# The gate stage's opening in a hybrid recurrent trunk: norm waits later in VectorE's queue, lifts one pair later, a fourth gate buffer

## The reference, cut to what matters

```python
out_a = _rms(o, gdn_norm_w) * silu(g_z)         # branch 0; 1 and 3 in the same way, 3 with a sigmoid
out_c = _rms(y * silu(s_z), ssd_norm_w)         # branch 2: gated first, then normed
branches = stack([out_a, out_b, out_c, out_d])  # each 256 wide
up    = einsum('btnw,nwd->btnd', branches, w_branch)        # the lift: 256 -> 1024, 4 branches
gates = sigmoid(gate.reshape(B, T, 4, 1024))                # gate = h @ w_in[:, C_GATE:]
merged = einsum('btnd,btnd->btd', gates, up)
y = merged @ w_out
```

## Time and profile before

| what | value |
|---|---|
| median of three executions | 1176.51 us (1175.53 to 1179.0) |
| the profiled execution, its own time | 1176.42 us |
| its span, first to last instruction | 1174.6 us |
| outside the span | 1.8 us |
| mean granted TensorE clock over the span | 0.961 of full |
| PE busy | 1101.2 us, 94% of the span |
| PE idle in the opening, 442.8 to 520.1 us | four waits, 13.5 us |
| DVE busy | 820.2 us, 70% |
| ACT busy | 458.2 us, 39% |

### The profile page before, as it was taken

How to read it: one execution, slowest core, us unless ns; L and a number is a source line. 1 busy time by engine, 2 the same in 40 slices (tenths; PEclk the granted TensorE clock), 3 DMA queues, 4 the chain that set the end, 5 groups by cost and what they waited for, 6 DMA issues and landing times.

```text
span 1174.6 us, 26651 instructions
## 1 busy us (share of the span) xinstructions
PE 1101.2 (94%) x11347; PEld 1029.5 (88%) x11347; DVE 820.2 (70%) x1464; ACT 458.2 (39%) x686; POOL 11.6 (1%) x29
## 2 busy tenths in 40 slices
PE   5889979999999999789999999979999999999997
PEld 3589978887667888789999999969999999999997
DVE  1647967778667865678888885586888889763433
ACT  2534495721102315763343332145444434541121
POOL 0001100000000000000000000000000000000000
PEclk9889999999869989989999999989999999999999
DMA  9924421112557216113333334222233333233201
GB/s 302 273 80 102 101 73 38 38 39 83 157 161 211 83 38 166 39 37 73 99 101 101 104 99 149 73 72 73 73 107 84 98 109 97 79 105 90 87 14 77
DMA packets 191052, 116.99 MB, mean 100 GB/s; under 512 B 36650, under 2 KB 189351, under 8 KB 190678
## 3 DMA queue, kind: packets, MB, share of 16 engines
q1 hardware_dynamic: 190358, 115.16, 34.7%
q0 software_dynamic: 576, 0.14, 0.1%
HBM read 108.31 MB, written 6.96 MB: 98 GB/s over the span
## 4 chain that ended last, share of the span: by engine, by line
PE 71%; DVE 6%; ACT 2%; issue 1%; DVEq 1%; ACTq 1%; PEldq 0%; PEld 0%
PE ps L924 70%; PE ps L928 1%; DVEq L2294 1%; DVE scr_parts L2992 1%; DVE pj L2274 1%; DVE pj_parts L3300 1%; ACTq L2123 0%; DVE scr L2706 0%; ACT rstd L1879 0%; DVE scr L2778 0%; DVE Vr L3254 0%; ACT scr_parts L2069 0%; DVEq L2275 0%; DVE scr L2953 0%; ACT scr L1989 0%
## 5 line engine op out<-in xcount | busy, mean ns | idle before, releaser
L924 PE MATMUL ps<-high_parts,scr_parts 128*128 128x272 f32 x1396 | 315.8, 297 | 22.4 <-DVE scr_parts L2992 9.5
L924 PE MATMUL ps<-hT_parts,scr_parts 128*128 128x272 f32 x960 | 263.3, 294 | 1.2 <-DVE pj_parts L3300 1.2
L924 PEld LDWEIGHTS ps<-high_parts,scr_parts 128*128 128x128 f32 x1396 | 239.4, 195 | 25.2 <-issue 12.7
L924 PE MATMUL ps<-pj_parts,scr_parts 128*128 128x272 f32 x1560 | 249.0, 289 | 0.3 <-issue 0.3
L924 PE MATMUL ps<-high_parts,ring_parts 128*128 128x272 f32 x812 | 238.6, 294 | 0.0
L924 PEld LDWEIGHTS ps<-pj_parts,scr_parts 128*128 128x128 f32 x1560 | 217.1, 188 | 0.7 <-issue 0.7
L924 PEld LDWEIGHTS ps<-hT_parts,scr_parts 128*128 128x128 f32 x960 | 179.1, 193 | 1.4 <-DVE scr_parts L2992 1.4
L924 PEld LDWEIGHTS ps<-high_parts,ring_parts 128*128 128x128 f32 x812 | 157.8, 194 | 0.7
L2992 DVE TENSOR_TENSOR scr_parts<-ring,scr_parts 128x1024 fp32r<-128x1024 f32 (+1 forms) x38 | 52.7, 1392 | 84.2 <-ACT scr_parts L2016 83.0
L2016 ACT ACTIVATE scr_parts<-ring 128x1024 fp32r<-128x1024 f32 (+1 forms) x38 | 44.9, 1191 | 142.6 <-PE ps L924 142.5
L924 PE MATMUL ps<-scr 64*64 64x64 f32 (+6 forms) x2352 | 80.4, 233 | 3.1 <-DVEq L2294 1.9
(11 more groups left out here) (424 smaller groups left out, 1820.3 us busy)
## 6 DMA issues: line engine op xcount, KB each, us to landing
ring<-in_w_in_dram SPq DMA_DIRECT2D x62, 512.0 KB, 5.1
ring<-in_ffn_w_in_dram SPq DMA_DIRECT2D x44, 512.0 KB, 5.2
ring<-in_ada_w_dram SPq DMA_DIRECT2D x40, 512.0 KB, 5.9
ring<-in_ffn_w_out_dram SPq DMA_DIRECT2D x16, 384.0 KB, 3.5
ring<-in_ffn_w_out_dram SPq DMA_DIRECT2D x16, 320.0 KB, 4.2
pj<-in_ada_w_dram SPq DMA_DIRECT2D x8, 512.0 KB, 8.3
ring<-in_w_out_dram SPq DMA_DIRECT2D x8, 512.0 KB, 4.2
x_scratch<-scr SPq DMA_DIRECT2D x1, 2176.0 KB, 12.2
```

The lines of the kernel that those rows point to most:

```text
L924: return pe.matmul(out, lhsT, rhs, start=start, stop=stop, skip_group_check=True)
```

## The change

It moves entries within the queues of ACT, DVE and PE, gives the gate pairs a fourth buffer, and lets the lifts follow one pair later. No matmul, split or product is added or left out.

- `high(0)` goes ahead of ACT's last `read_group`, `low(0)` ahead of DVE's `g_outc11`, and PE waits for the last copy (`x_read`) itself before `product(0)`.
- On ACT the loop over products 0 to 5 is written out: `T4_hi` goes ahead of `high(5)`; the logarithms of branches 0 and 1 are both taken ahead of both exponentials; `high(7)`, `high_a(0)`, `gate_out(1)` and `high_s(0)` stand ahead of the logarithms of branch 3; the exponentials of branches 2 and 3 follow together. The four silus of the z tiles go behind `gate_out(3)`.
- On DVE each `branch_squares` goes behind more splits, `branch_scaled(2)`, `branch_scaled(3)` and all `branch_gated` go into units 0 and 1, so that only `T3_lo` is left behind the splits of unit 0.
- On PE no lift follows unit 0, lifts 2s - 2 and 2s - 1 follow unit s, eight instead of six lifts follow unit 13. `sigmoid_a(0)` waits for no branch, `sigmoid_a(1)` for two.
- Two tiles are split to high and low during units 4 and 6, four (2 to 5) behind unit 13; before, four during units 3, 5, 7 and 9.

```diff
-MERGED, MERGED_HI = [0, 1, 2, 3, 6, 7, 8, 9], [14, 15, 16, 17, 28, 29, 4, 5]
+MERGED, MERGED_HI = [0, 1, 2, 3, 6, 7, 8, 9], [28, 29, 20, 21, 24, 25, 4, 5]
...
-            return ((pj[:, 10, :], pj[:, 11, :]), (Er[:, :], Vr[:, :]), (pj[:, 28, :], pj[:, 29, :]))[p % 3]
+            return ((pj[:, 10, :], pj[:, 11, :]), (Er[:, :], Vr[:, :]), (pj[:, 16, :], pj[:, 17, :]), (pj[:, 14, :], pj[:, 15, :]))[p % 4]
...
+            pe.wait_ge(x_read, GROUPS)
             for k in range(M_WOUT):
...
             for s in range(SG):
                 unit(s)
-                lift(2 * s)
-                lift(2 * s + 1)
-            for j in range(2 * SG, 4 * KD):
+                if s:
+                    lift(2 * s - 2)
+                    lift(2 * s - 1)
+            for j in range(2 * SG - 2, 4 * KD):
                 lift(j)
...
+                if engine == "act" and chain == "x" and name == "read":
+                    if t == GROUPS - 1:
+
+                        rest.after(act, NT, "m_normc")
+                        hgrn.after(act, PAIRS[-1], "h_outc1")
+                        high(0)
+                    read_group(t)
...
             def sigmoid_a(s):
-                if s == 0:
-                    act.wait_ge(branch_ready, 4)
-                else:
-                    act.wait_ge(lin_read, 2 * s)
+                if s == 1:
+                    act.wait_ge(branch_ready, 2)
+                elif s:
+                    act.wait_ge(lin_read, 2 * s - 2)
...
+            high(2)
+            z_out(0)
+            high(3)
+            z_out(1)
+            act.wait_ge(t_ready, 1)
+            act.activation(g_T2_hi, g_T2_raw, ACT.Copy).then_inc(t_high, 1)
+            act.activation(g_T1_hi, g_T1_raw, ACT.Copy).then_inc(t_high, 1)
+            high(4)
+            z_out(2)
+            norm_logs(0)
+            act.wait_ge(t_ready, 2)
+            act.activation(g_T4_hi, g_T4_raw, ACT.Copy).then_inc(t_high, 1)
+            high(5)
+            z_out(3)
+            norm_logs(1)
+            norm_exps(0)
+            norm_exps(1)
+            high(6)
+            gate_out(0)
+            norm_logs(2)
+            high(7)
             high_a(0)
+            gate_out(1)
             high_s(0)
+            norm_logs(3)
+            norm_exps(2)
+            norm_exps(3)
 
             act.wait_ge(first_scaled, 1)
             gate_out(2)
             high_b(0)
             high_s4(0)
-            for z in (GZ, GZ + 1, HG, HG + 1):
-                act.activation(pj[:, z, :], pj[:, z, :], ACT.Silu).then_inc(z_ready, 1)
             act.wait_ge(w_done, M_WOUT)
...
             gate_out(3)
+            for z in (GZ, GZ + 1, HG, HG + 1):
+                act.activation(pj[:, z, :], pj[:, z, :], ACT.Silu).then_inc(z_ready, 1)
...
+                    if (chain, t, name) == ("g", PAIRS[-1], "g_outc11"):
+
+                        low(0)
                     next(gens[chain])
...
             low(4)
+            branch_squares(1)
+            low(5)
             branch_squares(2)
-            branch_scaled(0)
-            low(5)
-            branch_squares(3)
             dve.wait_ge(t_high, 3)
             dve.tensor_tensor(g_T4_lo, g_T4_raw, g_T4_hi.bitcast(F32), SUB).then_inc(t_split, 1)
+            branch_scaled(0)
+            low(6)
             branch_scaled(1)
             sums(0)
-            low(6)
-            branch_scaled(2)
+            branch_squares(3)
             low(7)
-            branch_scaled(3)
...
+                if s == 0:
+                    branch_gated(0)
+                    branch_gated(1)
+                elif s == 1:
+                    for n in (2, 3):
+                        branch_scaled(n)
+                        branch_gated(n)
+                if s:
+                    gate_times_lift(2 * s - 2)
+            for k in range(2 * SG - 3, 4 * KD):
                 gate_times_lift(k)
-            merged_low(4)
-            gate_times_lift(4 * KD - 1)
-            merged_low(5)
+                if k < 2 * SG + 1:
+                    merged_low(k - 2 * SG + 5)
```

More of the change, by code:

```diff
@@ L1990, in rest_act @@
                         yield
[L1992 to L1999, removed]
             def high(m, at=None, n_at=None):
@@ L2016, in high @@
                 act.activation(hi, src, ACT.Copy).then_inc(w_split_hi, 1)
-            rest.after(act, NT, "m_normc")
-            hgrn.after(act, PAIRS[-1], "h_outc1")
-            high(0)
+            gens = {"g": gdn_act(), "h": hgrn_act(), "s": rest_act()}
+            for chain, t, name, engine in order:
+                if engine == "act" and chain == "x" and name == "read":
[4 more added lines that the diff above has]
+                    read_group(t)
+                elif engine == "act" and chain == "x":
+                    weights_high(t, int(name[-1]))
+                elif engine == "act":
+                    next(gens[chain])
             high(1)
@@ L2103, in sigmoid_a2 @@
                 act.activation(sw_gate(s)[:, halves[1]], sw_gate(s)[:, halves[1]], ACT.Sigmoid).then_inc(gate_sig, 1)
[L2105 to L2129, removed]
@@ L2130, in _, with norm_logs, norm_exps @@
-            act.drain()
+            def norm_logs(n):
+                mid.begin(act, 0, f"o_rs{n}")
+                for f in range(2):
+                    act.activation(two(rms[n][f]), ps[:, 4 + 2 * f:6 + 2 * f, 0:HN], ACT.Ln,
+                                   scale=1.0 / (P if n == 2 else DK), bias=colp[:, 3:4])
+                act.drain().then_inc(mid_s, 1)
+            def norm_exps(n):
+                for f in range(2):
+                    act.activation(rms[n][f], rms[n][f], ACT.Exp, scale=-0.5)
+                act.drain().then_inc(rms_ready, 1)
@@ L2157, in _ @@
                     high(M_WOUT + 1)
-                if s % 2 == 1 and 3 <= s < 11:
-                    merged_high((s - 3) // 2)
+                if s in (4, 6):
+                    merged_high((s - 4) // 2)
                 sigmoid_b(s)
                 sigmoid_a2(s)
-            act.wait_ge(lin_read, 4 * KD - 2)
-            merged_high(4)
-            merged_high(5)
+            act.wait_ge(op_done, 7 * (SG - 1) + 6)
+            for d in range(2, 6):
+                merged_high(d)
             act.wait_ge(lin_done, 4 * KD - 3)
@@ L2969, in rest_dve, with low @@
                         yield
+            def low(m, at=None):
+                _, src = piece(m)
+                hi, lo = parts(m)
+                dve.wait_ge(w_split_hi, (m if at is None else at) + 1)
+                dve.tensor_tensor(lo, src, hi.bitcast(F32), SUB).then_inc(w_split, 1)
             gens = {"g": gdn_dve(), "h": hgrn_dve(), "s": rest_dve()}
@@ L2985, in _ @@
             done(mid)
[L2987 to L2992, removed]
             def freed(s, j):
@@ L3121, in whole @@
                 tt(out, h_hi[:, k, c].bitcast(F32), h_lo[:, k, c].bitcast(F32), ADD)
-            low(0)
             low(1)
@@ L3135, in _ @@
             low(3)
-            branch_squares(1)
             dve.wait_ge(q_out["mlstm"], 64)
@@ L3161, in _ @@
             low_a(0, upper, 4)
[L3162 to L3167, removed]
+            for n in range(2):
+                at = slice(2 * n, 2 * n + 2)
+                dve.wait_ge(t_high, 4 + n)
+                dve.tensor_tensor(T3_lo[:, at, :], g_T3_raw[n], T3_hi[:, at, :].bitcast(F32), SUB).then_inc(t_split, 1)
             def merged_low(d):
@@ L3195, in _ @@
                 prepare = s + 1 < SG
-                if s:
-                    gate_times_lift(2 * s - 1)
+                if s >= 2:
+                    gate_times_lift(2 * s - 3)
                 if prepare:
@@ L3218, in _ @@
                     low_a(s + 1, upper, 4)
[L3219 to L3222, removed]
+                if s in (4, 6):
+                    merged_low((s - 4) // 2)
+                if s == 0:
[8 more added lines that the diff above has]
+            for k in range(2 * SG - 3, 4 * KD):
                 gate_times_lift(k)
-            merged_low(4)
-            gate_times_lift(4 * KD - 1)
-            merged_low(5)
+                if k < 2 * SG + 1:
+                    merged_low(k - 2 * SG + 5)
             mid.begin(dve, 0, "upc")
```

## The result

The changed kernel takes 1166.97 us (median of nine executions, 1162.95 to 1170.86) beside 1177.57 us for the kernel before (nine executions, 1169.56 to 1182.46): the ratio is **0.9914, interval 0.9885 to 0.9942**. The profiled execution took 1166.01 us with a span of 1164.2 us; before it was 1176.42 and 1174.6. The forecast was 1165.8 us, 0.991 of the kernel before.

The account below looks back on a forecast made before the run. PE's matmuls, plus time PE stands or runs slow, were taken as the bound. Losses of 19.2 us fall to 0.5 + 1.5 + 6.0 + 0.6 = 8.6; gain 10.6 from 1176.42 gives 1165.8 us, range 1162.5 to 1170.5.

Parts of the forecast that it names:

- The loss before (19.2 us): Opening of the stage, kernel before: four PE waits, 13.5 us, plus 5.7 us of low clock behind them.
- Start, 0.5 us left: Ahead of `product(0)`: 0.5 of the 2.69 us PE wait remains, too short to lower the clock.
- Products 4 and 6, no wait: Ahead of products 4 and 6: PE's waits of 2.65 and 4.15 us go, splits covered by at least 5 us.
- T3_lo, 1.5 us: Unit 0, after its second seventh: PE waits 1.5 us for `T3_lo` in place of 4.0.
- Units 0 to 2, 6.0 us: DVE late for PE in units 0 to 2: 6.0 us of new waits, including 0.5 for hand-overs.
- The clock in these waits, 0 taken: Units 0 to 2: 0 us for clock falls; up to 4.2 us kept in the range; clock 0.50 would show it wrong.
- Tail, 0.6 us: Lifts at the stage's end: merged splits on DVE make lift 30 late by 0.6 us.
- A, the forecast: Whole kernel: the forecast holds, 1162.5 to 1169 us; chance 0.65.
- B (clock): Units 1 and 2: the clock falls and is not absorbed, whole kernel 1170 us; chance 0.15.
- C (the backlog hardly shows): Units 1 and 2: PE never waits for DVE there, gain 16.6 us, 1159.8 us; chance 0.08.
- E (waits only change places): Ahead of `low(5)`: the serial chain squares, sums, logarithm holds DVE, losses return, 1176.4 us; chance 0.03.
- F (DVE never catches up): Units 3 to 13: every unit waits for `third_side`; 1185 us at a DVE period of 16 us; chance 0.03.

Follow-up runs that it names:

- e5: Changed kernel with each norm's exponentials directly behind its logarithms on ACT, three table loads more; 1166.99 us, ratio to before 0.9895.
- e2: Changed kernel with `high(0)` and `low(0)` moved back to their old places, PE still waiting for the last copy; 1169.46 us, ratio to before 0.9955.
- e4: Changed kernel with lifts 2s and 2s+1 behind unit s as before, DVE's `gate_times_lift` two earlier; 1171.28 us, ratio to before 0.9947.
- e7: Changed kernel with `branch_scaled(2)`, `(3)` ahead of `low_b(0)` and `branch_gated(0)` moved behind `up_second(1)`; 1163.46 us, ratio to before 0.9848.
- e9: Changed kernel with `branch_scaled(2)`, `(3)`, all `branch_gated` ahead of `T3_lo`, silus ahead of `T3_hi`, lifts 2s, 2s+1 behind unit s; 1169.45 us, ratio to before 0.9942.
- e6: Changed kernel with `branch_scaled(2)` and `(3)` taken out of unit 1 and put ahead of `low_b(0)` on DVE; 1164.04 us, ratio to before 0.9866.

## Why the prediction was right, and what it mis-sized

**What bounds and where: right.** The sum was a gain of 10.6 us; the stage gave 9.76, and the profiled executions 10.4, of which 0.3 each lie ahead of the stage and behind it.

**The loss before (19.2 us): right, at most 0.5 too low.** The four waits are as read. The clock was taken at 1.4 us for each. The start alone gave 3.58 us for 2.69 - 0.49 = 2.20 of wait, so 1.4 for one fits. From the start of `product(0)` to that of unit 0's second seventh PE took 68.96 us before (445.51 to 514.47) and 57.76 after (442.99 to 500.75): 11.20 less, for two waits of 6.80, so 4.4 us for three falls of the clock.

**Start, 0.5 us left: right** (0.49, clock 1.00).

**Products 4 and 6, no wait: right,** and the cover was as large as said: `low(5)`, `low(6)` and `low(7)` end at 471.7, 479.8 and 487.5. Even three table loads more (`e5`) brought no wait there.

**T3_lo, 1.5 us: 1.01.** ACT's walk ended at 501.21 us (501.3 said) and DVE's at 503.33 (503.6).

**Units 0 to 2, 6.0 us: the right size, by parts that were not.** The printed waits are 0.36 + 1.72 + 2.45 = 4.5. The rest is in waits too short to be printed. From the start of the second seventh of unit 0 to that of unit 1 (500.75 to 513.75) PE took 13.0 us, and seven sevenths (10.6) with the two printed waits (1.4) make 12.0. One result after another is handed over just too late. The fifth seventh of unit 0 waits for ACT's `copy_first(0)`, which ends at 506.56, and starts 0.15 us later; at 0.126 us a matmul the fourth would have let it start at 506.53, and the profile prints no wait:

```profile
505.02 1.67 PE L924 MATMUL ps<-scr_parts 128*128 128x272 f32 x12
...
506.19 0.37 ACT L2091 ACTIVATE rstd<-ps 128x272 f32<-128x272 f32 x1
...
506.71 0.36 PE L924 MATMUL ps<-high_parts,scr_parts 128*128 128x272 f32 x1
```

From unit 1 to unit 2 another 0.4 us is missing (16.32 us between the second sevenths, for 14.2 + 1.72). My 0.5 for hand-overs should have been 1.4, while the printed waits came to less than I had worked out.

**The clock in these waits, 0 taken: the step that failed.** It fell behind the wait of 2.45 us and cost 1.8: 18.46 us lie between the second sevenths of units 2 and 3, against 14.2 + 2.45, and the two windows above account for 2.50 x 0.27 + 2.80 x 0.37 = 1.7 of it.

```profile
530.07 1.68 PE L924 MATMUL ps<-scr_parts 128*128 128x272 f32 x12
...
548.53 1.67 PE L924 MATMUL ps<-scr_parts 128*128 128x272 f32 x12
```

The granted clock was 0.50 from 540 to 542 us, which the prediction had listed among the signs of being wrong. The argument that slower sevenths only shorten the next wait did not hold, since this was the last wait. The bound of 1.4 us for a fall was also too low.

**Tail, 0.6 us: 0.24.** It is lift 30 that is held, as said.

**The sum after** is then 0.5 + 1.0 + 4.5 + 1.4 + 1.8 + 0.2 = 9.4 us in place of 8.6, and 19.2 - 9.4 = 9.8 is what the stage gave. The failed step adds 1.8 us and the waits that came out smaller take 1.0 back. That the forecast came within 1.2 us of the measured median is in part luck: the executions of the changed kernel alone spread over 8 us.

**The table loads.** In the changed kernel ACT starts an exponential 1.29 us after its load starts:

```profile
472.59 1.28 ACT L2118 ACT_TABLE_LOAD   x1
473.88 0.66 ACT L2118 ACTIVATE Er<-Er 128x544 f32<-128x544 f32 x1
```

**The rivals.** A, the forecast, came true. B (clock) came true in one wait of three. C (the backlog hardly shows) is refuted by 4.5 us of printed waits. E (waits only change places) is refuted by products 4 and 6. F (DVE never catches up): no wait of PE lies between unit 2 and the last lifts.

## What to carry to other kernels

Work that an engine does in the shadow of another's wait is not free to move: when the wait goes, list what that engine must do until its next hand-over, beside what the bound engine does in the same stretch; the difference is the new wait, here 4.5 us, and the places where the helping engine still stands (3.56 us at `low_b(0)`) are where to put the work. Order a helper's queue by when each result is needed, and do not put a product's operand behind a serial chain that passes through a third engine. In this kernel PE's waits in the stage of up to 1.72 us kept the clock and those of 2.45 us and more lost it, all but one, at 1.4 to 1.8 us each (2.3 behind the one of 9.6); so a single long wait is worth removing before the same total in short ones.

## What the runs showed of the hardware

**The same length of wait does not always cost the clock.** It fell behind waits of 2.65 and 2.69 us, behind 2.78 us in `e2`, and in three profiles behind the 2.45 us; it stayed at 1.00 behind 2.77 us in `e4`. The Trainium skill (page "TensorE: Matmul & The Clock Gate", section "Part 1: The HAM clock gate") says that the window in which PE's activity is watched is free-running and does not reset when a kernel starts, and explains with it why the first matmuls of a kernel reach full speed at a varying point. That the place of a wait decides in the same way is not shown here: the runs would allow it, but in `e4` other work, too, stands around the wait (lifts follow it, not a seventh).

**The profile's idle time of PE is too short.** In the sevenths matmuls start 0.126 us apart but are drawn 0.29 us long, so 0.16 us of each stop is hidden under the last one's modelled end. A stall below that is not printed at all; distances between equal landmarks show it.

**The spread of executions goes with the mixers' clock.** The granted clock from 200 to 440 us, in `e7`, the changed kernel and `e9`, whose mixers ended at 451.4, 442.5 and 438.1 us:

```profile
200.00:440.00 240.00, 227.63 (x4449) 187.50 (x4450) 170.09 (x388) 66.58 (x123) 0.00 (x0) 0.88 0.34 99
```

```profile
200.00:440.00 240.00, 226.76 (x4592) 188.25 (x4590) 175.01 (x404) 65.13 (x122) 0.00 (x0) 0.91 0.34 99
```

```profile
200.00:440.00 240.00, 226.18 (x4625) 188.26 (x4624) 177.58 (x408) 67.72 (x124) 0.00 (x0) 0.94 0.34 100
```

The program of the mixers is the same in all three kernels, and their end spreads over 13 us. In all eleven profiles the two go together: clock 0.94, end at 438.1 and 440.4 us; 0.91, 441.7 to 447.0; 0.90, 446.5; 0.88, 450.8 and 451.4. This is why `e6` and `e7` were profiled in spans of 1168.6 and 1168.7 us although their stages are 4 to 5 us shorter than the changed kernel's; what sets the clock there was not tried.
